# Attention with keys and values per head, pairs on array halves, and the causal mask added by the tensor engine

## The reference, cut to what matters

```python
def mla_queries(x_n, pos, w_dq, q_norm, w_uq, w_uk):
    q = (rmsnorm(x_n @ w_dq, q_norm) @ w_uq).reshape(b, t, N_HEADS, QK_NOPE + QK_ROPE)
    q_lat = jnp.einsum('bthn,chn->bthc', q[..., :QK_NOPE], w_uk)
    q_rope = rope(q[..., QK_NOPE:], pos)
...
    for c, kr, mask in segments:
        s = (jnp.einsum('bqhc,bkc->bhqk', q_lat, c)
             + jnp.einsum('bqhr,bkr->bhqk', q_rope, kr)) * SOFTMAX_SCALE
        if mask is not None:
            s = jnp.where(mask, s, NEG_INF)
    p = jax.nn.softmax(jnp.concatenate(scores, axis=-1), axis=-1)
...     o_lat = sum over segments of p @ c
    return jnp.einsum('bqhc,chv->bqhv', o_lat, w_uv)
```

## Time and profile before

| | us |
|---|---|
| median of 3 runs | 2198.94 (2198.38 to 2200.59) |
| the profiled execution | 2198.22 |
| its span | 2196.4 |
| busy in the span: PE, DVE, ACT, POOL | 2109.1, 1427.7, 1009.0, 883.7 |
| mean granted clock of PE | 0.980 of full |

### The profile page before, as it was taken

One profiled execution on the slowest core, in us unless ns is written; L12 is line 12 of the kernel. 1 busy time (PEld: TensorE's weight loads), 2 busy tenths in 40 slices (PEclk: granted clock), 3 DMA queues, 4 the chain that ended last, 5 costly groups with the idle time before them and its releaser, 6 DMA issues.

```text
span 2196.4 us, 41571 instructions
## 1 busy us (share of the span) xinstructions
PE 2109.1 (96%) x13138; PEld 1846.2 (84%) x13138; DVE 1427.7 (65%) x3369; ACT 1009.0 (46%) x2085; POOL 883.7 (40%) x738
## 2 busy tenths in 40 slices
PE   7989999999999999997899998999999999999997
PEld 5769999999998888885674367999999998888886
DVE  4432996777768878872153203499577776887886
ACT  2535556444445555551252214555644445555554
POOL 0036998666652212200000005699866663221220
PEclk9989999999999999999999899999999999999999
DMA  4334555444469978863132624455544447897883
GB/s 153 108 125 129 188 182 182 144 143 138 139 228 311 316 258 302 288 219 123 55 97 88 190 97 144 135 182 183 178 137 143 139 138 277 310 311 259 297 288 123
DMA packets 125770, 408.81 MB, mean 186 GB/s; under 512 B 14626, under 2 KB 32514, under 8 KB 124802
## 3 DMA queue, kind: packets, MB, share of 16 engines
q1 hardware_dynamic: 103968, 333.76, 44.5%
q0 software_dynamic: 18432, 67.12, 10.3%
q10 hardware_dynamic: 3298, 7.08, 0.9%
HBM read 405.65 MB, written 1.66 MB: 185 GB/s over the span
## 4 chain that ended last, share of the span: by engine, by line
PE 32%; issue 13%; POOL 7%; DVE 1%; ACT 0%; POOLq 0%; ACTq 0%; DVEq 0%
PE ps L516 16%; POOL lo L1459 7%; PE ps L425 4%; PE ps L426 3%; PE ps L424 3%; PE ps L492 3%; PE ps L585 2%; PE ps L395 1%; PE ps L595 1%; PE ps L370 0%; DVE RT L1033 0%; POOLq L1458 0%; DVE X L1037 0%; ACTq L939 0%; DVE XN L1037 0%
## 5 line engine op out<-in xcount | busy, mean ns | idle before, releaser
L748 ACT ACTIVATE hi<-raw 128x512 fp32r<-128x512 f32 x1088 | 656.0, 626 | 491.0 <-PE ps L426 491.0
L1459 POOL TENSOR_TENSOR lo<-raw,hi 128x512 fp32r<-128x512 f32 x576 | 742.7, 1293 | 236.9 <-ACT hi L748 193.9
L424 PE MATMUL ps<-XH,hi 128*128 128x256 f32 (+1 forms) x2304 | 664.3, 288 | 21.6 <-POOL lo L1459 19.7
L425 PE MATMUL ps<-XL,hi 128*128 128x256 f32 (+1 forms) x2304 | 659.2, 286 | 0.0
L426 PE MATMUL ps<-XH,lo 128*128 128x256 f32 (+1 forms) x2304 | 655.4, 284 | 0.0
L424 PEld LDWEIGHTS ps<-XH,hi 128*128 128x128 f32 x2304 | 441.0, 191 | 24.7 <-POOL lo L1459 11.4
L425 PEld LDWEIGHTS ps<-XL,hi 128*128 128x128 f32 x2304 | 439.6, 191 | 0.0
L426 PEld LDWEIGHTS ps<-XH,lo 128*128 128x128 f32 x2304 | 435.3, 189 | 0.0
L516 PE MATMUL ps<-hi,WH 128*128 128x512 f32 x1024 | 398.3, 389 | 0.0
L516 PE MATMUL ps<-hi,WL 128*128 128x512 f32 x1024 | 398.3, 389 | 0.0
L516 PE MATMUL ps<-lo,WH 128*128 128x512 f32 x1024 | 398.3, 389 | 0.0
(11 more groups left out here) (246 smaller groups left out, 2226.9 us busy)
## 6 DMA issues: line engine op xcount, KB each, us to landing
raw<-in_stream SPq DMA_DIRECT2D x592, 512.0 KB, 3.4
pkeys<-in_pool SPq DMA_DIRECT2D x64, 192.0 KB, 3.2
plat<-in_pool SPq DMA_DIRECT2D x64, 128.0 KB, 2.2
SK<-in_sk ACTq DMA_DIRECT2D x2, 1024.0 KB, 5.5
X<-in_x SPq DMA_DIRECT2D x1, 1152.0 KB, 5.7
out_y<-X SPq DMA_DIRECT2D x1, 1152.0 KB, 4.2
wg<-in_wg ACTq DMA_DIRECT2D x1, 1024.0 KB, 10.4
rows<-in_u_rows,SE POOLq DMA_INDIRECT x64, 5.5
```

What stands on the lines that cost most here:

```text
L424: pe.matmul(ps[s][:, 0:n], h, XH[:, c, 0:n], start=c == 0, stop=False)
L425: pe.matmul(ps[s][:, 0:n], h, XL[:, c, 0:n], start=False, stop=False)
L748: act.activation(hi[k % 4][:], raw[s][:, half * HALF:(half + 1) * HALF], ACT.Copy)\
L1459: pool.tensor_tensor(lo[k % 4][:], raw[k // 2][:, half], hi[k % 4][:].bitcast(F32), ALU.subtract)\
```

## The change

- **Keys and values per head for the prompt.** Behind `norm(4)` PE now computes `KN`, the keys of all heads (16 matmuls with `wukn`, 256 columns), and `VV`, the values (8 matmuls, 512 columns). ACT copies `KN` from PSUM (8 copies), DVE copies `VV` (4 copies). `q_lat` is computed for the 32 sample tokens alone (32 matmuls of 32 columns), and ACT writes it straight to `QLS` (4 copies). `v_up` too runs on the sample tokens alone; the prompt's output comes from `VV` directly and DVE copies it to `AO`.
- **Pairs on halves.** The unit of the prompt is a `duo`: 4 heads for the second block of queries, 8 for the first; 6 duos in all. Within it two heads of a pair stand on the two row halves (scores, 64 rows each, in two PSUM banks) and on the two column halves (values). The rotated part takes 64 rows: the query halves times cosine and sine (`QROT`), against the key `KR`, which is computed on all 128 partitions. The sample attention takes two sequences at once, 64 columns each, in 4 steps.
- **The mask by PE.** A matmul with the unit matrix as weights adds `causal` to the scores in PSUM, for each head; DVE takes the maximum of 512 columns straight from PSUM, and ACT the exponential of each head.
- **Memory and loads.** There are four page buffers in place of two and two. A page comes as a DMA of 128 x 512 and one of 32 x 128 numbers, 16 for a sequence. Sequences 0 and 1 are loaded ahead of the tiles of `w_dq`, 2 and 3 ahead of those of `w_o`, and 4 to 7 behind the first four tiles of `w_o`, as each pair of buffers comes free (`pv_done`).
- The input of `w_dq` has a buffer of its own (`XM`) and is written before the rotated key. `load_mla` has nine DMAs in place of seven, the page table first.

```diff
+                def load_pages(b):
+                    numbers = [sp.value_load(...) for n in range(b * NPAGES, (b + 1) * NPAGES)]
+                    x = b % 4
+                    if b >= 4:
+                        sp.wait_ge(pv_done, DUOS + (b - 4) // 2 + 1)
+                    for j, number in enumerate(numbers):
+                        sp.dma_start(pg[x][:, j, 0:2 * LAT], page[:, 0:2 * LAT]).then_inc(page_in[x], 16)
+                        sp.dma_start(pg[x][0:ROPE, j, 2 * LAT:], page[0:ROPE, 2 * LAT:]).then_inc(page_in[x], 16)
+                if phase == "w_dq":
+                    sp.wait_ge(table_in, 16)
+                    load_pages(0)
+                    load_pages(1)
...
             norm(4)
+            pe.wait_ge(mla_in, 16 * MLA_LOADS)
+            for t in range(HEADS // 2):
+                if t >= 2:
+                    pe.wait_ge(k_evac, t - 1)
+                for c in range(LC):
+                    mm = pe.matmul(out[:, 0:SEQ], wukn[:, c, t * P:(t + 1) * P], CT[:, c, 0:SEQ], ...)
+            pe.wait_ge(proj_evac, EVAC["w_dq"] + 4)
+            for kb in range(2):
+                for half in range(2):
+                    for c in range(LC):
+                        mm = pe.matmul(ps[2 * kb + half][:], CT[:, c, kb * P:(kb + 1) * P],
+                                       wuv[:, c, half * 512:(half + 1) * 512], ...)
...
+            def d_scores(d):
+                for i in range(ns):
+                    for par in range(2):
+                        pe.matmul(out, QN[r, h // 2, q], KN[r, h // 2, 0:kk], start=True, stop=False)
+                    for par in range(2):
+                        pe.matmul(out, QRC[r, h // 2, q], KR[r, 0:kk], start=False, stop=False)
+                    for par in range(2):
+                        mm = pe.matmul(out, ident[:], causal[:], start=False, stop=True)
...
+            d_scores(0)
+            d_scores(1)
+            for d in range(DUOS):
+                d_turn(d)
+                if d + 2 < DUOS:
+                    d_scores(d + 2)
+                d_values(d)
...
+            s_scores(0)
+            s_scores(1)
+            for j in range(DB // 2):
+                s_turn(j)
+                s_values(j)
+                if j + 2 < DB // 2:
+                    s_scores(j + 2)
+                s_back(j)
...
+            d_max(0)
+            d_max(1)
+            for d in range(DUOS):
+                d_norm(d)
+                if d + 2 < DUOS:
+                    d_max(d + 2)
+                if d >= 1:
+                    d_out(d - 1)
```

More of the change, by code:

```diff
@@ L344, in _ @@
                     load(t0 + s, s)
+                if phase == "w_o":
+                    for b in range(4, DB):
+                        load_pages(b)
                 if count > SLOTS:
@@ L692, in _ @@
[L692 to L701 removed]
+            pe.wait_ge(proj_evac, EVAC["q_lat"])
@@ new lines, in _ @@
+            for c in range(LC):
+                for h in range(HEADS):
+                    r = slice(NOPE * (h % 2), NOPE * (h % 2) + NOPE)
+                    mm = pe.matmul(ps[2 * c + h % 2][:, NSAMP * (h // 2):NSAMP * (h // 2 + 1)],
+                                   wuk[r, h // 2, c * P:(c + 1) * P], QN[r, h // 2, SEQ:TOK], start=True, stop=True)
+                    if h >= HEADS - 2:
+                        mm.then_inc(proj_done, 1)
+            pe.wait_ge(qr_ready, 1)
+            pe.wait_ge(proj_evac, EVAC["q_lat"] + 4)
@@ new lines, in _ @@
+            pe.wait_ge(ol_ready, DB // 2)
+            for k in range(HEADS // 2):
+                for c in range(LC):
+                    for par in range(2):
+                        h = 2 * k + par
+                        mm = pe.matmul(ps[0][VH * par:VH * par + VH, NSAMP * k:NSAMP * (k + 1)],
+                                       wuv[:, c, h * VH:(h + 1) * VH], OL[:, c, h, :], start=c == 0, stop=c == LC - 1)
+            mm.then_inc(proj_done, 1)
+            pe.wait_ge(ao_ready, DUOS)
@@ new lines, in _ @@
+                act.dma_start(QR[:].rearrange("r a (i h) n -> r a h i n", h=2)[:, part, par],
+                              QRC[ROPE * q:ROPE * (q + 1), :, SEQ:TOK]).then_inc(qr_in, 16)
+            for p in range(4):
+                c, par = divmod(p, 2)
+                act.wait_ge(proj_done, PLAIN["q_lat"] + p + 1)
+                act.activation(QLS[:, c].rearrange("p b (i h t) -> p h i b t", h=2, t=DS)[:, par],
+                               ps[p][:, 0:SEQ].rearrange("p (i b t) -> p i b t", b=DB, t=DS), ACT.Copy)\
+                    .then_inc(proj_evac, 1)
@@ new lines, in d_exp @@
+            def d_exp(d):
+                qb, ns, heads = duo(d)
+                kk = P * (qb + 1)
+                act.wait_ge(nm_ready, d + 1)
+                if d >= 2:
+                    act.wait_ge(pt_done, 2 * (d - 2) + 2)
+                for par in range(2):
+                    x = 2 * (d % 2) + par
+                    for i in range(ns):
+                        ins = act.activation(PP[x][:, i * kk:(i + 1) * kk], ps[x][:, i * kk:(i + 1) * kk], ACT.Exp,
+                                             bias=stat[:, d % 2, 1, 4 * par + i:4 * par + i + 1], scale=SCALE,
+                                             accum_out=stat[:, d % 2, 2, 4 * par + i:4 * par + i + 1])
+                    ins.then_inc(p_exp, 1)
@@ L1365, in _ @@
             scaled(CQN, CQ, G_Q, QC, xn_ready)
+            for k in range(4):
+                kb, half = divmod(k, 2)
+                dve.wait_ge(vv_done, k + 1)
+                dve.tensor_copy(VV[:, kb, half * 512:(half + 1) * 512], ps[k][:]).then_inc(vv_evac, 1)
             for t in range(4, 8):
@@ L1485, in _, with duo @@
                     fetch(n)
-SC_BANK = (0, 1, 6)
-MLA_LOADS = 7
+MLA_LOADS = 8
+DUOS = 6
+def duo(d):
+    qb, ns, first = (1, 2, 4 * d) if d < 4 else (0, 4, 8 * (d - 4))
+    return qb, ns, [[first + 2 * i + par for i in range(ns)] for par in range(2)]
 AT_EXP = 12
```

567 lines of the change are left out of this document (271 added, 296 removed).

## The result

The changed kernel takes 2192.44 us (median of 8 runs, 2189.20 to 2196.37), the kernel before 2199.41 on the same chip (2198.38 to 2200.79): a ratio of 0.997, interval 0.9961 to 0.998. A second series on another chip gave 2191.92 against 2195.89, 0.9987 (0.9978 to 0.9996). So the change is worth 0.1 to 0.3%, where 1% was forecast; the time lies 1.4 us above the forecast's range. The profiled execution took 2195.76 us, with a span of 2193.9.

A forecast was written before the change was run, and what follows sets the result against it. The prediction took PE, in its own program order, to bound each stage; -1.0 + 7.0 - 12.1 - 13.3 + 1.1 - 3.6 + 1.7 = -20.2 us off the profiled 2198.22 gave 2178.0, range 2154 to 2191.

The forecast's parts named there:

- To the end of `norm(4)`: Stretch ending at 1043.24: fewer transposes and copies save 1.0 us, `w_dq` tile landing about 1021; ends -3 and +6.
- Keys, values and `w_uq`: Key and value matmuls after `norm(4)`, partly covering PE's wait for `CQN`: 39.15 becomes 46.1 us, +7.0.
- Queries: From the queries to the first scores: 64 records of 32 columns and copies take 6.0 instead of 18.08 us, -12.1.
- Prompt attention: Paired heads with waits take 48.1 us, plus 10.2 for the clock: 58.3 instead of 71.57, -13.3.
- six stretches of 1.7: Prompt attention: PE's idling brings six stretches at the lower clock, 1.7 us each, 10.2 in all; bounds 0 and 20.
- Sample attention: Pairs halve PE work, but two page load waits of 23.9 us eat the gain: 113.6 instead of 112.52, +1.1.
- Value projection: 64 small records at 0.069 us each, 4.4 us, and 0.5 for the copy, against 8.53: -3.6.
- `w_o`: Output projection behind the attention: it starts after low activity, so the lower clock costs +1.7 us.
- that the clock holds: Rival, attention stages and `w_o`: idling need not lower the clock, so 10.2 + 10.2 + 1.7 come off: 2156; chance 0.22.
- that halves don't pair: Rival, prompt attention: row halves don't run side by side, costing 10.4 us more: 2188; chance 0.08.
- a queue ahead of `w_dq`: Rival, before `norm(4)`: page and constant transfers queue up ahead of `w_dq`, up to +6 instead of -1: 2185; chance 0.13.
- SP's issues: Rival, `w_dq` and sample attention page loads: every second of 96 issues stalls by 0.7 us, +34: 2212; chance 0.05.

The follow-up runs named there:

- e6: Changed kernel with the pages of sequences 0 and 1 issued behind the first four `w_dq` tiles instead of ahead of them: 2184.46 us, 0.9963 of the kernel before.
- c1: The changed kernel unaltered, measured again on another chip as base for the follow-up runs: 2191.92 us, 0.9987 of the kernel before.
- e1: Changed kernel with only ACT's order altered in the sample attention, copies of turned probabilities ahead of the next pair's exponentials: 2176.76 us, 0.9918 of the kernel before.
- e8: Changed kernel with each prompt head's matmuls one behind the other, so no two array halves stand side by side: 2231.94 us, 1.0151 of the kernel before.
- e14: Changed kernel with 40 unread matmuls of 64 rows, alternating between row halves, in each sample attention load wait: 2191.01 us, 0.9965 of the kernel before.
- e2: Changed kernel with pair 1's values ahead of pair 2's scores on PE, later pairs finished singly, ACT's order matched: 2154.59 us, 0.9828 of the kernel before.
- e13: Changed kernel with 20 unread matmuls of 64 rows, all on one row half, in each sample attention load wait: 2192.44 us, 0.9967 of the kernel before.
- e9: Changed kernel with 24 unread matmuls of 128 rows and 512 columns in each sample attention load wait: 2191.90 us, 0.9986 of the kernel before.
- e4: Changed kernel with each page fetched by one transfer of 128 x 640 instead of two: 2174.66 us, 0.9921 of the kernel before.

## Why the prediction was off

Step by step, by its own parts.

- **To the end of `norm(4)`, -1.0:** -0.8. The tile was asked for at 1018.55 and PE started at 1021.08; the forecast had 1021. Right, and in its size. It took over as given that `w_dq` runs slowly behind such a wait, as it did before; e6 shows what that costs.
- **Keys, values and `w_uq`, +7.0:** +7.3. Right.
- **Queries, -12.1:** -12.1. Right (5.98 us for 6.0).
- **Prompt attention, -13.3:** -11.9. Mechanism right: at the full clock the turns take 7.6 and 9.3 us where the forecast worked out 7.6 and 9.4; in e6 the second of these is the distance of these two lines of `d_turn`:

```profile
1119.17 1.46 PE L650 MATMUL ps<-ident,PP 128*128 128x128 f32 x8 [1.69 <-DVE PP L1464]
...
1128.49 1.46 PE L650 MATMUL ps<-ident,PP 128*128 128x128 f32 x8 [1.69 <-DVE PP L1464]
```

  PE idles 1.7 us in such a turn, not 3; two masks take 0.64 us and not 0.45. What the stage takes beyond the forecast's 48.1 of work and waits, there 10.2 for the clock, is 11.6 us in this execution and 8.2 in c1. It did not come in six stretches of 1.7: in this execution four cost some 2.9, 1.6, 1.5 and 4.5 us (an estimate, by what the same records take at the full rate). That the total fits is partly luck.
- **Sample attention, +1.1: the step that failed.** +16.7. The load waits are right (24.25 and 24.08 for 23.9). The terms as written add up to 114.7, since one copy back stands at 1.4 where 113.6 needs 0.3; that slip of 1.1 is not what failed. The sum put 1.6 us between a turn and its values and 0.3 between the copy back and the next turn, that is the bare copies, as in the earlier trace rows, where one sequence's work was done before the next one's began. It didn't look at ACT's program, in which `s_exp(j + 2)` stands ahead of `s_back(j)` and `s_exp(1)` ahead of `s_turn(0)`. It named the queue behind each wait on PE and on SP, not on ACT. The three waits are 9.1 us over what they are in e1. The clock makes another 4.5 of the difference to the forecast, in the scores and turns. With ACT's order changed the stage is 112.5, the forecast's 113.6, and the whole 0.9918 (0.9899 to 0.9936), 18 us, where the forecast had 20.2. That this agrees so well is partly luck: the forecast had the values of all four pairs at 5.8 us, and in e1 they took 4.3 at the full clock, 6 us less together, while the scores behind the first load were 2.9 us slower, and the loads and the copies back together 2.6 us longer, than its terms.
- **Value projection, -3.6:** -5.7. The term of 69 ns a record was mis-sized: 64 records take 2.32 us, 36 ns each, with a granted clock of 0.79, and 2.06 us in c1. That the pairs on column halves overlap here would fit it, but no run takes them apart. The Trainium skill, TensorEngine Tiling, Performance Considerations ("Instruction Overhead"), has an overhead of some 60 cycles for a matmul, the same for 1 column as for 60; by estimate that is 25 ns at 2.4 GHz. In this stage the records lie nearer to it than to the row's 69 ns, among the queries (64 in 3.76 us, 59 ns) nearer to the row.
- **`w_o`, +1.7:** +4.0. `w_o` itself takes 47.88 us instead of 45.14, 2.7 of it in its first 48 records, and what follows is 1.2 longer. The term for the clock, 1.7, was too small; the stage ahead had a granted 0.68.

The rivals: that the clock holds is refuted (0.81 and 0.68 in the attention), that halves don't pair by e8 and e14, a queue ahead of `w_dq` by its start at 1021. SP's issues did not stall (0.51 to 0.52 us apart, but for single ones). None of them was the case; the range was too narrow on the slow side since its upper end came from them alone, and no case had another engine's order in it.

## What to carry to other kernels

Where work on one engine is halved by pairing, write down for each engine, the idle ones too, what its program has ahead of the copy that the bounding engine waits for next: an engine that is busy for a tenth of a stage can hold up another by its order alone, and a wait can be paid twice, once as itself and once in the clock behind it (9.1 and 8.0 us here, 2.5 and 2.5 in e6). Buffers that are freed by the last step of a pair want that step ahead of the next pair's first one, so that two loads can follow one another. A mask that bfloat16 holds well enough took TensorE a third of its time in float32 here (0.21 for 0.64 us a pair).

## What the hardware showed that was not expected

- A gap can be paid twice: 2.53 us of waiting for a tile made the next 64 records of 288 columns take 18.19 us instead of 15.68 (e6). It need not be: behind 1.31 us the same 32 records took 3.67 us in e1 and 5.36 in e2.
- The first scores, started at the lower clock, were back at the full one after 6 us when two heads ran side by side, and not in 22 us when each ran alone (e8); yet a later stretch of paired scores stayed low for 11 us. Started at the full clock, 17.4 us of work on one half kept it (e13).
- Filling a wait of 24 us with 20.9 us of idle matmuls gave 3.3 us of the stage and nothing measurable of the time (e9).
- SP issues a transfer with a computed address every 0.51 to 0.52 us and takes 4.9 us for eight numbers and what lies between; transfers of 320 KB at that pace land after 5.5 us instead of 2.9 for those of 256 and 16 KB (e4).
- Records of 32 columns on alternate column halves start 36 ns apart at a granted clock of 0.79 (64 in 2.32 us); in c1, where 64 take 2.06 us, 32 ns.
